# Differential softmax on one core: the order of the next head's scores and the step's gate piece on TensorE

## The reference, cut to what matters

```python
def blocked_attention(q, k, v, scale):
    def attend(qi):
        s = jnp.einsum('bkgqd,bksd->bkgqs', qi, k, preferred_element_type=jnp.float32) * scale
        p = jax.nn.softmax(s, axis=-1).astype(v.dtype)
        return jnp.einsum('bkgqs,bksv->bkgqv', p, v)
...
def diff_branch(zl, zc, ...):
    ...
    def combine(o):
        o = o[:, 0] - lam.astype(o.dtype) * o[:, 1]
        return merge_heads(rms_norm(o, subln) * (1.0 - lam_init))
...
def merge_branches(ys, gate_logits, w_branch, w_out):
    g = jax.nn.sigmoid(gate_logits.reshape(b, t, N_BRANCH, D_MODEL))
    m = g[:, :, 0] * (ys[0] @ w_branch[0])
    for i in range(1, N_BRANCH):
        m = m + g[:, :, i] * (ys[i] @ w_branch[i])
    return m @ w_out
```

## Time and profile before

| | |
|---|---|
| median of 3 runs | 2621.41 us (2620.99 to 2621.75) |
| the profiled execution | 2624.72 us |
| its span in the trace | 2622.9 us |
| TensorE busy | 2508.6 us (96%) |
| VectorE, ScalarE, GpSimd busy | 1356.2, 759.5, 1490.3 us |
| stage of the differential softmax, layer 0 | about 701 to 828 us |
| the same, layer 1 | about 2026 to 2130 us |

### The profile page before, as it was taken

One profiled execution on the slowest core, in us unless ns is written; L12 is line 12 of the kernel. 1 busy time (PEld: TensorE's weight loads), 2 busy tenths in 40 slices (PEclk: granted clock), 3 DMA queues, 4 the chain that ended last, 5 costly groups with the idle time before them and its releaser, 6 DMA issues.

```text
span 2622.9 us, 37769 instructions
## 1 busy us (share of the span) xinstructions
PE 2508.6 (96%) x15408; PEld 2090.7 (80%) x15408; DVE 1356.2 (52%) x1807; ACT 759.5 (29%) x1276; POOL 1490.3 (57%) x1375
## 2 busy tenths in 40 slices
PE   4999999999999999999999999999999999999998
PEld 2798888877777888888877889887777768888877
DVE  3632156543477877555565464326754778421241
ACT  4611333432255511111120033133532564111200
POOL 3443458523423636666669616547835445788896
PEclk9999999999999999999999999999999999999999
DMA  7422422312412843444434354222321346333332
GB/s 277 143 85 88 122 59 67 90 51 83 105 57 91 278 119 104 125 129 118 124 102 120 113 171 145 76 54 81 81 61 50 98 135 211 113 96 97 88 95 82
DMA packets 379489, 287.32 MB, mean 110 GB/s; under 512 B 10565, under 2 KB 339625, under 8 KB 378806
## 3 DMA queue, kind: packets, MB, share of 16 engines
q1 hardware_dynamic: 376896, 281.97, 35.9%
q10 hardware_dynamic: 1814, 2.85, 0.3%
q0 software_dynamic: 608, 0.09, 0.0%
HBM read 253.42 MB, written 29.36 MB: 108 GB/s over the span
## 4 chain that ended last, share of the span: by engine, by line
PE 78%; DVE 11%; POOL 4%; ACT 3%; DMA 2%; issue 2%; ACTq 1%; SPq 0%; DVEq 0%; POOLq 0%
PE ps L558 18%; PE ps L559 17%; PE ps L560 17%; PE ps L1309 3%; PE ps L787 3%; POOL w_lo L1469 2%; PE ps L608 2%; PE ps L609 2%; PE ps L610 2%; DVE ffl L2607 2%; ACT arena L1796 2%; PE ps L914 1%; PE ps L1245 1%; PE ps L818 1%; PE ps L855 1%
## 5 line engine op out<-in xcount | busy, mean ns | idle before, releaser
L1466 POOL TENSOR_TENSOR w_hi<-ring,tiny 128x512 fp32r<-128x512 f32 x480 | 541.1, 1127 | 947.1 <-PE ps L560 537.5
L1469 POOL TENSOR_TENSOR w_lo<-ring,w_hi 128x512 fp32r<-128x512 f32 (+1 forms) x568 | 800.5, 1413 | 78.0 <-ACT w_hi L1674 40.4
L558 PE MATMUL ps<-hh,w_hi 128*128 128x512 f32 (+1 forms) x2288 | 829.1, 362 | 14.8 <-DVE hl L2157 9.8
L559 PE MATMUL ps<-hl,w_hi 128*128 128x512 f32 (+1 forms) x2288 | 807.0, 353 | 0.0
L560 PE MATMUL ps<-hh,w_lo 128*128 128x512 f32 (+1 forms) x2288 | 806.3, 352 | 0.0
L558 PEld LDWEIGHTS ps<-hh,w_hi 128*128 128x128 f32 x2288 | 434.5, 190 | 110.4 <-issue 32.1
L560 PEld LDWEIGHTS ps<-hh,w_lo 128*128 128x128 f32 x2288 | 434.1, 190 | 60.4
L559 PEld LDWEIGHTS ps<-hl,w_hi 128*128 128x128 f32 x2288 | 435.1, 190 | 55.3 <-issue 0.5
L1969 ACT ACTIVATE arena<-ps,vec 128x768 f32<-128x768 f32 (+1 forms) x44 | 39.1, 888 | 424.8 <-PE ps L560 424.8
L1796 ACT ACTIVATE arena<-ps,tiny,vec 128x768 f32<-128x768 f32 (+1 forms) x120 | 108.7, 906 | 181.9 <-DVE tiny L2337 181.8
L2616 DVE SCALAR_TENSOR_TENSOR arena<-ps,vec,arena 128x511 f32<-128x511 f32 x66 | 43.6, 660 | 220.5 <-ACT arena L1969 219.8
(11 more groups left out here) (277 smaller groups left out, 3811.6 us busy)
## 6 DMA issues: line engine op xcount, KB each, us to landing
ring<-in_w_in SPq DMA_DIRECT2D x118, 512.0 KB, 4.1
ring<-in_w_mod SPq DMA_DIRECT2D x96, 512.0 KB, 3.9
ring<-in_w_up SPq DMA_DIRECT2D x88, 512.0 KB, 4.1
ring<-in_w_down SPq DMA_DIRECT2D x48, 512.0 KB, 3.6
ring<-in_w_out SPq DMA_DIRECT2D x32, 512.0 KB, 3.7
logits<-arena SPq DMA_DIRECT2D x32, 384.0 KB, 2.6
arena<-logits SPq DMA_DIRECT2D x32, 384.0 KB, 4.5
ring<-in_w_down SPq DMA_DIRECT2D x24, 384.0 KB, 3.1
```

The lines of the kernel that those rows point to most:

```text
L558: pe.matmul(acc, wh[:, offset + k], hi[:, n, x:y], start=n == 0, stop=False)
L559: pe.matmul(acc, wh[:, offset + k], lo[:, n, x:y], start=False, stop=False)
L1466: pool.tensor_tensor(wh[:, 0:count], w, one[:].unsqueeze(2).to_broadcast([P, count, P]), ALU.mult).then_inc(*up("w_lead", ("lead", key, j)))
L1469: pool.tensor_tensor(wl[:, 0:count], w, wh[:, 0:count].bitcast(F32), ALU.subtract).then_inc(*up("w_split", ("split", key, j)))
```

## The change

In every step of the differential softmax the gate pieces of the step are issued on TensorE ahead of the scores of the next head, where they were issued behind them. The turning of the step's weights still comes after both. The order of the grouped-query softmax, which shares the loop, stays as it was, since only the scores of the differential branch stand in front of the gate pieces.

```diff
@@ -927,9 +927,9 @@
                 for part in early_parts(l, b)[len(early_parts(l, b)) // 2:]:
                     gate_part(l, part)
                 for n, (t, h) in enumerate(order):
+                    among(l, b, n)
                     if b == "dif" and n + 1 < len(order):
                         scores(*order[n + 1])
-                    among(l, b, n)
                     if b == "gqa" and n % 2 == 1 and n + 1 < len(order):
                         scores_of_pair(n + 1)
                     base[("oT", l, b, t)] = base[("o", l, b, t)] = 5 * 512 + 256
```

## The result

The changed kernel takes 2649.33 us (median of 4 runs, 2648.63 to 2650.11); beside it the kernel before takes 2621.58 us. The ratio is 1.0098 with an interval of 1.0086 to 1.0111: **27.7 us slower**, where 10 were forecast and 17.6 was the top of the range. The sign was right, the size was not.

What follows compares the result with a forecast made beforehand. TensorE bounds the kernel, busy 2508.6 of 2622.9 us. Waits for the difference (+12.5) less saved exponential waits (9.5) give +3, collisions +7: 2621.4 + 10 = 2631.4 us, range 2624 to 2639.

Steps and rivals of the forecast that it cites:

- the order alone: Differential softmax on TensorE: 12.5 us lost waiting for the difference, 9.5 saved waiting for exponentials, net +3 us.
- collisions with GpSimd: VectorE's difference meets GpSimd's weight splitting after a gate piece, now on TensorE's path: +7 us.
- The score waits: Score matmuls (L876, L894) waiting for an exponential (ACT L1796): from 13.7 to 4.2 us, 9.5 saved.
- The turn waits: Turning of the weights (L914) waiting for the difference (DVE L2367): from 3.0 to 15.5 us without collisions, some 22 overall.
- the walk through the chain: Step-by-step count of both softmax stages from single-row durations; in the old order it gave 124 and 100 us.
- ten of twelve at 0.7 us: Of twelve waiting steps in both layers, ten have the difference let in some 0.7 us later by GpSimd: +7 us.
- The row that the forecast priced: L2366 at 2055.88 in layer 1, 1.33 us instead of 0.22, ending as GpSimd's w_lo does.
- heavy collisions: Rival: GpSimd meets both L2366 and L2367, twelve times at 1.1 us or more: +16 us, 2637.4 us, chance 0.14.
- L2366 stretched at even steps: Sign expected in the new trace: VectorE's L2366, 0.22 us when free, takes longer at even steps; no size given.

Runs made afterwards that it cites:

- pool_later: The changed kernel, but GpSimd splits the next weights only when the step's difference is done; 2627.36 us, ratio 1.0017 to the kernel before.
- fill_half: The changed kernel with useless matmuls (nine at most per step) on TensorE ahead of long waits for the difference; 2641.96 us, ratio 1.0073 to the kernel before.
- the second one: Profiled execution of a rerun of the changed kernel, unaltered; the rerun took 2653.23 us, ratio 1.0104 to the kernel before.

## Why the prediction was right in sign and wrong in size

Put together, from the stages of the profiled executions, in us:

| term | forecast | measured | from |
|---|---|---|---|
| the order alone | +3 | +2.0 | `pool_later` against before |
| collisions with GpSimd | +7 | +15.8 (13.6 by the waits) | `fill_half` against `pool_later` |
| TensorE's clock | 0 | +10.0 (12.2 by busy time) | the changed kernel against `fill_half` |
| sum | +10 | +27.8 | |

The figures in brackets are a second way to the same sum. Of the 27.8 us, 15.6 are more waiting and 12.2 are more busy time of the same matmuls; `pool_later` waits 2.0 us more than the kernel before, which leaves 13.6 to the collisions.

**The score waits** went from 13.7 to 2.7 us, none in layer 1: right (4.2 forecast, and 3.7 where nothing else disturbs). **The turn waits** without collisions: right, 15.0 against 15.5 us. The bottleneck, the direction and the walk through the chain held, with its durations from single rows. The turn waits as they came, 29.6 us in 18 places, were forecast as some 22 in some 20. What also held is the statement that the collisions lie hidden in the old order, and that no matmul waits for weights: no L558 is among the waits of TensorE's matmuls.

**The mis-sized term is "ten of twelve at 0.7 us".** I counted how much later the first GpSimd instruction lets VectorE in, 1.35 in place of 0.5 us after the piece, and took the difference to be free from then on. But GpSimd's two instructions follow each other within 0.1 us, and the second takes its turn against L2367. In layer 1 this happened at six of the seven steps that wait (1, 4, 6, 10, 12, 14): 3.0 to 3.3 us a difference in place of 1.47, and 2.2 us at step 2. The turn waits were 10.9 us longer than without collisions (16.9 against 6.0), 1.6 us a step. In layer 0 the differences of steps 1, 8, 12 and 22 were longer by 0.8, 0.8, 1.5 and 0.7 us. The places were forecast right but for one (step 2 of layer 0 was not hit in this execution), the price was that of half of the event. The whole event stood in the trace of the kernel before, at step 13 of layer 0 (timeline, VectorE and GpSimd only), where it cost TensorE nothing:

```profile
777.49 1.05 POOL L1466 TENSOR_TENSOR w_hi<-ring,tiny 128x512 fp32r<-128x512 f32 x1
777.54 0.16 DVE L2365 RECIPROCAL tiny<-tiny 128x1 f32<-128x1 f32 x1 [1.22 <-ACT arena L1796]
777.74 0.81 DVE L2366 SCALAR_TENSOR_TENSOR tiny<-tiny 128x1 f32<-128x1 f32 x1
778.59 2.12 DVE L2367 SCALAR_TENSOR_TENSOR arena<-arena,tiny 128x768 f32<-128x768 f32 x1
778.62 1.28 POOL L1469 TENSOR_TENSOR w_lo<-ring,w_hi 128x512 fp32r<-128x512 f32 x1
```

That is 3.17 us for one difference, where GpSimd starts its pair as VectorE sets out. The row that the forecast priced from the earlier trace rows has VectorE meet only the second instruction, so that L2367 went free. The forecast did see the double hit, but gave it to the rival "heavy collisions" at 1.1 us, 16 us in all, with a chance of 0.14. Its collision term was the right one, or nearly: 13 us plus the feedback. What would have told the two apart, beside that row, is the length of the two GpSimd instructions together, 2.4 us, against the 1.47 us of the difference that begins with them: it can't get through between.

What the forecast named as a sign, "L2366 stretched at even steps", was no sign: its mean is 552 ns before and 557 after. L2367's went from 1088 to 1542.

**The step that was missing is the clock.** The sum adds waits one for one. That holds for a kernel whose clock stays, and the earlier trace rows show 1.00; but they show it for waits of at most 1.6 us, and the forecast itself had turn waits of 2 us or more. The changed kernel's clock fell to 0.50 behind two pairs of waits of 1.3 to 1.5 us, each pair ending 2.4 us apart (717.4 and 719.8, 758.6 and 761.0), and behind single ones of 2.2 us and more, though not behind each. The matmuls that follow then take up to twice as long. That the waits are what lowers it is shown by `pool_later` (waits at most 1.6 us: 1.00) and by `fill_half` (the same collisions with little of the idling: 1.00). The Trainium skill, "TensorE: Matmul & The Clock Gate", section "What's actually happening", says that the clock is halved by default, that activity releases it, and that 1.2 and 2.4 GHz are its two states. By that rule, the trace agrees: the short stretches above show 0.50, 0.51 or 1.00, and 0.91 or 0.97 are mixtures. It should have been a rival for a change that moves idle time of TensorE into fewer and longer pieces, with a price: by the window of 6.20 us at 0.51, an estimate of 3 us lost behind one pair of waits, as much as the pair itself (1.33 + 1.49 us).

**The range** reached to 2639 us, the bound of a collision at L2366 only, with nothing for the clock. With L2367 blocked as well and the clock it had to reach 10 to 14 us further.

Left open: what decides whether one wait of 2.5 us lowers the clock. In layer 1 three executions of the new order with turn waits of 16.9, 16.9 and 15.7 us got clocks of 0.97, 0.94 and 0.90. And the exact split between collisions and clock in layer 0. In layer 1 the added matmuls of `fill_half` ended before the difference at the six steps that have nine of them (0.2 to 0.4 us of wait is left at each), and both ways of counting agree to half a microsecond (collisions 10.5 or 10.9 us, clock 3.3 or 2.9). In layer 0 no wait is left at most of the filled steps, so the matmuls may end late there, and `fill_half` has a collision at step 2 that the changed kernel didn't have (2.44 us in place of 1.47). There the counts are 5.3 or 2.7 us for the collisions and 6.7 or 9.3 for the clock. So the collisions cost 13.6 to 15.8 us and the clock 10.0 to 12.2 in this execution; in the second one, where the waits are the same, the clock took some 5 us more.

## What to carry to other kernels

A wait that is moved to another place isn't the same wait: ask what starts at the same event (here the end of the gate piece, which frees GpSimd just as VectorE sets out), and count the whole burst that it starts, not its first instruction. Where TensorE is 95% busy and its waits grow beyond what the trace of before contains, the granted clock is a term of the sum, not a constant. And where two waits compete for one piece of cover, split the piece before choosing a side: half on each side, with GpSimd held back until the difference is done, took the stage from 126.1 and 102.4 to 122.2 and 99.1 us.

## What the runs showed of the hardware that I had not expected

- TensorE's clock halves inside a kernel whose TensorE is 95% busy. Two waits of about 1.4 us close together stood ahead of it in the two cases shown, where it then lasted 6.2 and 5.6 us, and it made up 10 to 12 us of a loss of 27.8. With useless matmuls in the gaps the kernel was 18.5 us slower than before the change, without them 27.7.
- A VectorE instruction recorded 0.03 us *before* GpSimd's is still held by it: L2367 at 2075.07 took 2.10 us beside w_lo at 2075.10, in place of 1.02. The Trainium skill, "SBUF — State Buffer", section "Who interferes with whom", has whichever comes second blocked for the whole of the first. That fits L2366 behind w_hi (2073.98), but by the recorded starts it does not fit this row; the start in the trace may not be the moment at which the two compete.
- It goes the other way as well. In layer 0, step 12 of the changed kernel (timeline):

```profile
785.15 1.04 POOL L1466 TENSOR_TENSOR w_hi<-ring,tiny 128x512 fp32r<-128x512 f32 x1
785.23 1.76 DVE L2367 SCALAR_TENSOR_TENSOR arena<-arena,tiny 128x768 f32<-128x768 f32 x1
786.26 1.86 POOL L1469 TENSOR_TENSOR w_lo<-ring,w_hi 128x512 fp32r<-128x512 f32 x1
```

L2367 is held by w_hi, and w_lo, which takes 1.27 us alone, is then held by L2367 (785.23 + 1.76 = 786.99) and ends at 788.12.
